# The chunked delta rule of one mixer: its 64x64 blocks held without their empty quarters

## The chip, the cores and the metric

The kernel runs on one core of a Trainium2 chip. The metric is device time in microseconds (us) from launch to the last byte written; lower is better. The kernel before took 2299.62 us, the median of three runs (2299.19 to 2301.99).

## The reference

Two models' blocks stand one behind the other on 512 tokens of width 1024, all in float32: four layers (pooling, short convolution, latent attention, pooling), then a hybrid mixer and a gated feed-forward layer. The change is in the mixer, in its gated delta rule: 4 heads, key and value size 128, chunks of 64 tokens.

```python
def gated_delta_rule(q, k, v, g, beta):          # chunks of C = 64 tokens, 8 chunks
    g = jnp.cumsum(chunks(g), axis=-1)
    decay = jnp.where(causal, jnp.exp(gdiff), 0.0)            # C x C for each chunk
    L = jnp.where(strict, einsum('bhnid,bhnjd->bhnij', k_beta, k) * decay, 0.0)
    rhs = jnp.concatenate([v * beta[..., None], k_beta * jnp.exp(g)[..., None]], axis=-1)
    sol = triangular_solve(L + jnp.eye(C), rhs, left_side=True, lower=True, unit_diagonal=True)
    u, w = sol[..., :dv], sol[..., dv:]
    a_intra = einsum('bhnid,bhnjd->bhnij', q, k) * decay
    ...
    def step(state, xs):                                      # 8 steps, one after the other
        v_new = u_c - w_c @ state
        o = qd_c @ state + a_c @ v_new
        state = state * jnp.exp(gl_c) + kd_c.T @ v_new
```

## The kernel before, in words

Every projection is a stream of tiles. A tile is 128 output features by 512 tokens: 24 TensorE products (L665 to L667) of 128x512, three for each of 8 blocks of a weight split into a high and a low part. SyncE loads the weights, ScalarE makes the high parts (L1212), GpSimd the low parts (L594), in a ring of four buffers. Each engine has its own instruction order, written out by hand; semaphores of the mixer count named steps (`mixer_steps`), and an engine waits for the count of the step that it needs.

In the mixer the delta rule works on pairs of chunks: 512 tokens are 4 blocks of 128 tokens, and each block's 128x128 matrix has two 64x64 chunk matrices on its diagonal and zeros in the other two quarters. One step handles one head: four blocks side by side, 128 partitions by 512 columns, one PSUM bank.

`delta_products` on TensorE sets groups of four heads between single projection tiles: `bg` spreads the summed gate over 128 partitions (L907), `vt` and `kt` turn values and keys (L914), `g1` is keys by scaled keys (L916), `g2` keys by queries (L916). VectorE makes the decay exponent from `bg` (L2004), ScalarE its exponential (L1456). VectorE multiplies `g1` into the lower matrix and takes from it the start of the inverse (L2021, L2023, L2024), and multiplies `g2` (L2030).

`inverse` then builds the inverse of the triangular matrix by doubling the block size from 2 to 64, levels 1 to 5. First `x1` turns `xt` (L914) and `bg2` spreads the gate again (L907). In each level and for each head TensorE makes `y` from `e_mat` and `x_mat` (L916, bank in `proj`); ScalarE copies it into `y_mat` (L1483); TensorE makes `p`, that is two products, one into `aux` and one into `proj` (L916); VectorE subtracts them from `x_mat` (L2046) and `xt` (L2048), and masks the next level's `e_mat` while `p` is under way (L2042). Level 5 has only the product into `aux` and no `e_mat`. `wt` multiplies `vf` by the inverse (L916), and ScalarE stores it negated (`nw`, L1495). No projection tile stands between the steps of `inverse`.

Last comes a loop over 8 chunks that is interleaved with two softmax attentions, all products in one TensorE order: attention scores (L1006), `new_values` (L1018 the inverse by the values, L1021 the product with the state, head by head in turn), turned probabilities (L1057), outputs (L1033, L1037), state update (L1043), attention values (L1071), sums (L1084).

A product in plain float32 is recorded as two weight loads and two matmuls; a "record" below is one of them. The projection's products, on split operands, are one record each, as are the turns at L914.

Of the kernel before, what the change touches and what calls it, by code (L numbers as in the profile page):

```python
# [24 lines left out]
P = 128  # L25
# [52 lines left out]
for _name, _n in (("levels", LEVELS * P), ("mask_t", P), ("dist", 4 * P), ("dist_swa", 2 * P)):  # L78
    CONSTS2[_name] = _at
    _at += _n  # L80
# [78 lines left out]
def mixer_steps():  # L159
# [10 lines left out]
    act += each("egl", "edt") + each("vb") + each("kd") + each("xc") + each("eg")  # L170
# [93 lines left out]
def program(nc, x_in, stream, params_in, consts_in, consts2_in, pos_in, out, phases):  # L264
    ctx = ExitStack()
    with ctx:
# [18 lines left out]
        x_mat = sb("x_mat", [P, 4, 4, P], F32, late)  # L285
        y_mat = sb("y_mat", [P, 4, 4, P], F32, late)
        e_mat = sb("e_mat", [P, 4, 4, P], F32, late)
        v_tok = sb("v_tok", [P, 4, 3, P], F32, late)
        eg = y_mat
# [81 lines left out]
        l_mat = kb.rearrange("p h (b k) -> p h b k", k=P)  # L371
# [14 lines left out]
        xt = sb("xt", [P, 4, 4, P], F32, over)  # L386
# [89 lines left out]
        def level(l):  # L476
            return consts2[:, l * P:l * P + P].unsqueeze(1).broadcast_to([P, 4, P])
# [4 lines left out]

        def decay_of(h):
            return blocks_of(decay[:, h, :])
# [159 lines left out]
        def _(pe):  # L644
# [273 lines left out]

            def tiles(n):
                for _ in range(n):  # L920
                    products(tile.n % BANKS, 8, of_x)

            def delta_products():
# [22 lines left out]
                for h in HEADS:  # L946
                    pe.wait_ge(mix_dve, DVE_STEP["kb", h])
                    made(spread_row(h, 0, 32 + h), ("bg", h))
                tiles(1)
                for h in HEADS:  # L950
                    pe.wait_ge(mix_act, ACT_STEP["egl", h])
                    made(per_block(h, 0, None, lambda blk: vf[:, h, blk * P:blk * P + P], turn=True), ("vt", h))
# [5 lines left out]
                for h in HEADS:  # L958
                    pe.wait_ge(mix_act, ACT_STEP["kd", h])
                    made(per_block(h, 0, lambda blk: kf[:, h, blk * P:blk * P + P],  # L960
                                   lambda blk: kb[:, h, blk * P:blk * P + P]), ("g1", h))
                tiles(1)
                for h in HEADS:
                    pe.wait_ge(mix_dve, DVE_STEP["lt", h])
                    made(per_block(h, 0, lambda blk: kf[:, h, blk * P:blk * P + P],
                                   lambda blk: qf[:, h, blk * P:blk * P + P]), ("g2", h))
                tiles(1)

            def inverse():

                for h in HEADS:
                    pe.wait_ge(mix_dve, DVE_STEP["at", h])
                    made(per_block(h, 0, None, lambda blk: xt[:, h, blk, :], turn=True), ("x1", h))
# [3 lines left out]
                for l in range(1, LEVELS):  # L977
                    for h in HEADS:
# [31 lines left out]
            def new_values(c):  # L1010
# [14 lines left out]
            def output_and_update(c, last_value):  # L1025
# [10 lines left out]
                for h in HEADS:  # L1036
                    mm = pe.matmul(banks(1)[:, h * CHUNK:h * CHUNK + CHUNK], vnew[r:r + CHUNK, h * P:h * P + P],  # L1037
                                   blocks_of(kf[:, h, :])[r:r + CHUNK, blk, r:r + CHUNK],
# [159 lines left out]
        def _(act):  # L1198
# [186 lines left out]
            def hybrid_mixer():  # L1385
# [88 lines left out]
                for h in HEADS:  # L1474
                    act.wait_ge(mix_pe, PE_STEP["x1", h])
                    made(act.activation(x_mat[:, h, :, :], blocks_of(head_bank(h, 0)), ACT.Copy), ("xc", h))
                for h in HEADS:
                    act.wait_ge(mix_pe, PE_STEP["bg2", h])
                    made(act.activation(eg[:, h, :, :], blocks_of(head_bank(h, 1)), ACT.Exp), ("eg", h))
# [13 lines left out]
                for h in HEADS:  # L1493
                    act.wait_ge(mix_pe, PE_STEP["wt", h])
                    made(act.activation(vf[:, h, :], head_bank(h, 0), ACT.Copy, scale=-1.0), ("nw", h))  # L1495
# [154 lines left out]
        def _(dve):  # L1650
# [256 lines left out]
            def hybrid_mixer():  # L1907
# [91 lines left out]
                mask_t = consts2[:, CONSTS2["mask_t"]:CONSTS2["mask_t"] + P]  # L1999
# [19 lines left out]
                for h in HEADS:  # L2019
                    dve.wait_ge(mix_pe, PE_STEP["g1", h])  # L2020
                    made(dve.tensor_tensor(l_mat[:, h, :, :], blocks_of(head_bank(h, 0)), decay_of(h), ALU.mult), ("lt", h))  # L2021

                    link(dve.tensor_tensor(xt[:, h, :, :], l_mat[:, h, :, :], level(0), ALU.mult))  # L2023
                    made(dve.scalar_tensor_tensor(xt[:, h, :, :], xt[:, h, :, :], -1.0,  # L2024
                                                  con("ident", P).unsqueeze(1).broadcast_to([P, 4, P]),
                                                  ALU.mult, ALU.add), ("xt0", h))
# [374 lines left out]
```

## Time and profile before

| what | us |
|---|---|
| profiled execution, its own time | 2300.2 |
| its span | 2298.4 |
| median of three runs | 2299.62 |
| TensorE matmuls busy | 2224.7 (97%) |
| VectorE busy | 1168.0 (51%) |
| ScalarE busy | 894.3 (39%) |
| GpSimd busy | 1066.4 (46%) |

In the rows below PE is TensorE's matmuls, PEld its weight loads, DVE is VectorE, ACT is ScalarE, POOL is GpSimd. A matmul row has the rows and columns of the array that it uses before its output's shape: `64*128` is 64 rows by 128 columns. Matmuls are pipelined, so the time that a matmul costs in a stream is the distance from its start to the next one's start, which is shorter than its own duration.

### The profile page before, as it was taken

What the parts mean: (1) busy time and instruction counts of PE and PEld (TensorE: products, weight loads), DVE (VectorE), ACT (ScalarE), POOL (GpSimd) and SP (SyncE); (2) the same over time, 40 slices, a digit from 0 to 9 for tenths busy, and PEclk for the clock granted to TensorE, in tenths of its full rate; (3) what the DMA queues carried; (4) which work ended last, traced back from release to release, by engine and by line L of the source; (5) the groups of instructions that cost most, each with busy time, mean ns of one, the idle gap of its engine ahead of it and who ended that gap; (6) DMA issues with size and microseconds to landing.
All of it is one profiled execution on the core that took longest, in us unless ns stands there. A gap on an engine that the chain in (4) does not pass through costs nothing.

```text
span 2298.4 us, 32107 instructions
## 1 busy us (share of the span) xinstructions
PE 2224.7 (97%) x10384; PEld 1799.7 (78%) x10384; DVE 1168.0 (51%) x1538; ACT 894.3 (39%) x1567; POOL 1066.4 (46%) x789
## 2 busy tenths in 40 slices
PE   8999999999999999999999999999999888999996
PEld 6788888888888887777787788878798666878885
DVE  7842234444432553555338523367684448888513
ACT  4243333434433344444332444334635433332322
POOL 5654444454454444444446544445302333555553
PEclk9999999999999999999999999999999889999998
DMA  3232322222222232111122322322200021223232
GB/s 136 92 110 91 101 92 101 91 100 94 98 97 95 97 101 75 63 56 56 65 92 92 101 98 94 101 98 92 71 22 1 1 73 56 91 91 100 101 109 92
DMA packets 53642, 194.45 MB, mean 85 GB/s; under 512 B 6080, under 2 KB 6336, under 8 KB 53568
## 3 DMA queue, kind: packets, MB, share of 16 engines
q1 hardware_dynamic: 52560, 191.13, 24.7%
q10 hardware_dynamic: 1008, 2.33, 0.3%
q8 instruction: 47, 0.77, 0.1%
q14 instruction: 27, 0.22, 0.0%
HBM read 191.34 MB, written 2.10 MB: 84 GB/s over the span
## 4 chain that ended last, share of the span: by engine, by line
PE 71%; issue 17%; POOL 9%; DVE 2%; ACT 1%; POOLq 0%; ACTq 0%; DVEq 0%
PE proj L665 18%; PE proj L666 18%; PE proj L667 18%; POOL w_lo L594 9%; PE aux L799 2%; PE proj L824 1%; PE proj L916 1%; PE aux L916 1%; PE proj L753 1%; PE proj L755 1%; PE proj L754 1%; PE aux L802 1%; PE aux L810 1%; PE proj L1018 0%; PE aux L1006 0%
## 5 line engine op out<-in xcount | busy, mean ns | idle before, releaser
L594 POOL TENSOR_TENSOR w_lo<-w_stage,w_hi 128x512 fp32r<-128x512 f32 x716 | 989.9, 1391 | 1029.0 <-ACT w_hi L1212 1028.3
L1212 ACT ACTIVATE w_hi<-w_stage 128x512 fp32r<-128x512 f32 x716 | 438.1, 627 | 770.1 <-PE proj L667 701.8
L665 PE MATMUL proj<-xh,w_hi 128*128 128x512 f32 x1696 | 671.2, 396 | 11.8 <-POOL w_lo L594 9.7
L666 PE MATMUL proj<-xl,w_hi 128*128 128x512 f32 x1696 | 662.7, 391 | 0.0
L667 PE MATMUL proj<-xh,w_lo 128*128 128x512 f32 x1696 | 662.4, 391 | 0.0
L665 PEld LDWEIGHTS proj<-xh,w_hi 128*128 128x128 f32 x1696 | 319.2, 188 | 94.2 <-POOL w_lo L594 22.2
L666 PEld LDWEIGHTS proj<-xl,w_hi 128*128 128x128 f32 x1696 | 319.5, 188 | 66.7 <-issue 2.4
L667 PEld LDWEIGHTS proj<-xh,w_lo 128*128 128x128 f32 x1696 | 319.4, 188 | 66.9
L665 PE MATMUL proj<-act_h,w_hi 128*128 128x512 f32 (+1 forms) x840 | 327.6, 390 | 0.6 <-POOL w_lo L594 0.6
L667 PE MATMUL proj<-act_h,w_lo 128*128 128x512 f32 (+1 forms) x840 | 327.3, 390 | 0.0
L666 PE MATMUL proj<-act_l,w_hi 128*128 128x512 f32 (+1 forms) x840 | 327.3, 390 | 0.0
L665 PEld LDWEIGHTS proj<-act_h,w_hi 128*128 128x128 f32 x840 | 157.8, 188 | 34.7 <-issue 1.0
L667 PEld LDWEIGHTS proj<-act_h,w_lo 128*128 128x128 f32 x840 | 157.8, 188 | 32.7
L666 PEld LDWEIGHTS proj<-act_l,w_hi 128*128 128x128 f32 x840 | 157.8, 188 | 32.3
L1289 ACT ACTIVATE act_h<-prod 128x512 f32 (+1 forms) x102 | 64.5, 632 | 257.7 <-DVE prod L2150 130.7
L1671 DVE TENSOR_TENSOR ssum<-ssum,sq 128x512 f32<-128x512 f32 x64 | 62.0, 969 | 152.2 <-ACT sq L1218 151.5
L1712 DVE TENSOR_TENSOR x_res<-proj,x_res 128x512 f32 x32 | 22.1, 692 | 218.4 <-PE proj L667 217.1
L1751 DVE TENSOR_TENSOR act_l<-prod,act_h 128x512 f32 (+1 forms) x102 | 82.0, 804 | 84.8 <-ACT act_h L1289 84.8
L2156 DVE TENSOR_TENSOR z<-proj,rstd 128x512 f32<-128x512 f32 x32 | 22.1, 692 | 112.7 <-PE proj L667 111.9
L632 POOL TENSOR_SCALAR probs<-probs,soft 128x256 f32<-128x256 f32 (+3 forms) x32 | 30.4, 962 | 105.3 <-DVE soft L2059 105.3
L608 POOL TENSOR_SCALAR pr<-pr,small 128x128 f32<-128x128 f32 (+3 forms) x32 | 40.8, 1274 | 76.1 <-DVE small L1851 76.1
L1336 ACT ACTIVATE pr<-aux,small 128x128 f32<-128x128 f32 (+3 forms) x64 | 33.2, 524 | 53.1 <-DVE small L1844 53.1
(311 smaller groups left out, 2427.7 us busy)
## 6 DMA issues: line engine op xcount, KB each, us to landing
w_stage<-stream SPq DMA_DIRECT2D x358, 512.0 KB, 3.3
out<-x_res SPq DMA_DIRECT2D x4, 512.0 KB, 2.6
x_res<-x SPq DMA_DIRECT2D x2, 512.0 KB, 8.7
consts_sb<-consts ACTq DMA_DIRECT2D x1, 832.0 KB, 4.5
x_res<-x ACTq DMA_DIRECT2D x1, 512.0 KB, 7.8
x_res<-x SPq DMA_DIRECT2D x1, 256.0 KB, 3.4
x_res<-x ACTq DMA_DIRECT2D x1, 256.0 KB, 5.4
pos_i<-pos ACTq DMA_DIRECT2D x1, 256.0 KB, 2.6
```

Of the source, the lines that this page charges most:

```text
L594: pool.tensor_tensor(w_lo[:, at, :], w_stage[:, at, :], w_hi[:, at, :].bitcast(F32), ALU.subtract).then_inc(stage_free, 1)
L608: pool.tensor_scalar(pr[:, qb % 2, 0, 0:w], pr[:, qb % 2, 0, 0:w], stat(INVERSE, qb)[:, 0:1], None, ALU.mult).then_inc(probs_done, 1)
L665: pe.matmul(o, w_hi[:, slot, cols], hi, start=(b == 0), stop=False)
L666: pe.matmul(o, w_hi[:, slot, cols], lo, start=False, stop=False)
L667: mm = pe.matmul(o, w_lo[:, slot, cols], hi, start=False, stop=(b == blocks - 1))
L799: pe.matmul(score_banks(qb, w)[:, h, :], qn[:, p % 2, h, q], kn[:, p % 2, h, 0:w], start=True, stop=False)
L916: mm = pe.matmul(o, stationary(blk), moving(blk), start=True, stop=True)
L1212: act.activation(w_hi[:, u % RING, :], w_stage[:, u % RING, :], ACT.Copy).then_inc(hi_done, 1)
L1289: act.activation(act_h[:, slot, :], prod[:, :], ACT.Copy).then_inc(ah_done, 1)
L1336: e = act.activation(pr[:, qb % 2, h, 0:w], score_banks(qb, w)[:, h, :], ACT.Exp, bias=stat(BIAS, qb)[:, h:h + 1], scale=SCALE, accum_out= ...
L1671: dve.tensor_tensor(total[:, :], total[:, :], sq[:, (sqs.n - 1) % 2, :], ALU.add).then_inc(ssum_done, 1)
L1751: dve.tensor_tensor(act_l[:, slot, :], prod[:, :], act_h[:, slot, :].bitcast(F32), ALU.subtract).then_inc(al_done, 1)
```

## The change

Each chunk's 64x64 matrix is now kept alone. Of a block of 128 tokens the first chunk lies on partitions 0 to 63 and the second on 64 to 127, both in the same 64 columns, so a head takes 128 partitions by 256 columns. `x_mat`, `y_mat`, `e_mat`, `xt`, the level masks and the decay have this half width. Every 128x128 product of these steps becomes two 64x64 products, one on each half of the partitions. `bg` is made in this form by two products; the decay exponent is made by two VectorE operations of 256 columns a head in place of four of 128. `x1` can no longer be one turn of a block and becomes products with an identity. `wt` multiplies each half into its own bank. The exponential of the chunk ends (`egl`) moves behind `bg2`, and `eg` has a buffer of its own. In the chunk loop the product of the inverse with the values reads 64 rows where it read 128.

```diff
+            def per_chunk(h, b, stationary, moving):
+                for blk in range(4):
+                    for r in (0, CHUNK):
+                        mm = pe.matmul(compact(head_bank(h, b))[r:r + CHUNK, blk, :], stationary(blk, r), moving(blk, r),
+                                       start=True, stop=True)
+                return mm
...
-                    made(spread_row(h, 0, 32 + h), ("bg", h))
+                    for r in (0, CHUNK):
+                        at = CONSTS["ident"] + 32 + h
+                        mm = pe.matmul(compact(head_bank(h, 0))[r:r + CHUNK, :, :],
+                                       consts[0:64, at:at + 1].broadcast_to([64, CHUNK]),
+                                       rows[0:64, :].rearrange("p (b r k) -> p b r k", r=2, k=CHUNK)[:, :, r // CHUNK, :],
+                                       start=True, stop=True)
+                    made(mm, ("bg", h))
...
-                    made(per_block(h, 0, lambda blk: kf[:, h, blk * P:blk * P + P],
-                                   lambda blk: kb[:, h, blk * P:blk * P + P]), ("g1", h))
+                    made(per_chunk(h, 0, tokens_of(kf, h), tokens_of(kb, h)), ("g1", h))
...
-                    made(per_block(h, 0, None, lambda blk: xt[:, h, blk, :], turn=True), ("x1", h))
+                    made(per_chunk(h, 0, chunk_of(xt, h), ident_of), ("x1", h))
...
-                        made(per_block(h, 1, lambda blk: e_mat[:, h, blk, :], lambda blk: x_mat[:, h, blk, :]), (f"y{l}", h))
+                        made(per_chunk(h, 1, chunk_of(e_mat, h), chunk_of(x_mat, h)), (f"y{l}", h))
...
-                        mm = per_block(h, 0, lambda blk: y_mat[:, h, blk, :], lambda blk: xt[:, h, blk, :])
+                        mm = per_chunk(h, 0, chunk_of(y_mat, h), chunk_of(xt, h))
                         if l < LEVELS - 1:
-                            mm = per_block(h, 1, lambda blk: xt[:, h, blk, :], lambda blk: y_mat[:, h, blk, :])
+                            mm = per_chunk(h, 1, chunk_of(xt, h), chunk_of(y_mat, h))
...
-                    made(per_block(h, 0, lambda blk: blocks_of(vf[:, h, :])[:, blk, :],
-                                   lambda blk: xt[:, h, blk, :]), ("wt", h))
+                    for blk in range(4):
+                        for i in range(2):
+                            r = CHUNK * i
+                            mm = pe.matmul(compact(head_bank(h, i))[:, blk, :], blocks_of(vf[:, h, :])[r:r + CHUNK, blk, :],
+                                           xt[r:r + CHUNK, h, blk, :], start=True, stop=True)
+                    made(mm, ("wt", h))
...
-                    mm = pe.matmul(o, xt[:, h, blk, r:r + CHUNK], vbeta[:, h, blk, :], start=(h == 0), stop=(c == 0),
+                    mm = pe.matmul(o, xt[r:r + CHUNK, h, blk, :], vbeta[r:r + CHUNK, h, blk, :], start=(h == 0), stop=(c == 0),
...
-                    made(act.activation(egl[:, h, :], head_bank(h, 0)[:, CHUNK - 1::CHUNK], ACT.Exp), ("egl", h))
-                    made(act.activation(decay[:, h, :], decay[:, h, :], ACT.Exp), ("edt", h))
+                    made(act.activation(decay_of(h), decay_of(h), ACT.Exp), ("edt", h))
...
-                        made(act.activation(y_mat[:, h, :, :], blocks_of(head_bank(h, 1)), ACT.Copy), (f"yc{l}", h))
+                        made(act.activation(y_mat[:, h, :, :], compact(head_bank(h, 1)), ACT.Copy), (f"yc{l}", h))
...
-                    for blk in range(4):
-                        ins = dve.scalar_tensor_tensor(decay_of(h)[:, blk, :], head_bank(h, 0)[:, blk * P:blk * P + P],
-                                                       cols[:, blk, 32 + h:33 + h], mask_t, ALU.subtract, ALU.add)
-                    made(ins, ("dt", h))
+                    link(dve.tensor_tensor(decay_of(h), compact(head_bank(h, 0)),
+                                           cols[:, :, 32 + h:33 + h].broadcast_to([P, 4, CHUNK]), ALU.subtract))
+                    made(dve.tensor_tensor(decay_of(h), decay_of(h), mask_t, ALU.add), ("dt", h))
```

On TensorE, at level 1 of the inverse, the program before has for one head the product `y` (`x_mat,e_mat`) and the two products of `p`:

```order
L916 MATMUL proj<-x_mat,e_mat 128x128 [waits mix_dve,mix_act]
L916 MATMUL proj<-x_mat,e_mat 128x128 x3
L916 MATMUL aux<-xt,y_mat 128x128 [waits mix_act]
L916 MATMUL aux<-xt,y_mat 128x128 x3
L916 MATMUL proj<-y_mat,xt 128x128 x4
```

The changed program has at the same place, its lines being L933:

```order
L933 MATMUL proj<-x_mat,e_mat 64x64 [waits mix_dve,mix_act]
L933 MATMUL proj<-x_mat,e_mat 64x64 x7
L933 MATMUL aux<-xt,y_mat 64x64 [waits mix_act]
L933 MATMUL aux<-xt,y_mat 64x64 x7
L933 MATMUL proj<-y_mat,xt 64x64 x8
```

Twelve products of 128x128 have become twenty-four of 64x64; the waits are the same.

On TensorE in the chunk loop, at chunk 1, the program before has between two score products (L1006) the new values, where `xt` and `vf` are the operands of the inverse and of the state:

```order
L1006 MATMUL aux<-a_kv,a_q 128x256
L1018 MATMUL proj<-vbeta,xt 64x128 [waits mix_dve]
L1021 MATMUL proj<-state,vf 64x128
L1018 MATMUL proj<-vbeta,xt 64x128
L1021 MATMUL proj<-state,vf 64x128
L1018 MATMUL proj<-vbeta,xt 64x128
L1021 MATMUL proj<-state,vf 64x128
L1018 MATMUL proj<-vbeta,xt 64x128
L1021 MATMUL proj<-state,vf 64x128
```

The changed program has the same order, its lines being L1045, L1057 and L1060:

```order
L1045 MATMUL aux<-a_kv,a_q 128x256
L1057 MATMUL proj<-vbeta,xt 64x128 [waits mix_dve]
L1060 MATMUL proj<-state,vf 64x128
L1057 MATMUL proj<-vbeta,xt 64x128
L1060 MATMUL proj<-state,vf 64x128
L1057 MATMUL proj<-vbeta,xt 64x128
L1060 MATMUL proj<-state,vf 64x128
L1057 MATMUL proj<-vbeta,xt 64x128
L1060 MATMUL proj<-state,vf 64x128
```

Nothing has moved here; what the rows don't show is that L1057 now reads 64 partitions where L1018 read 128, while L1060 reads 128 as L1021 did.

## Rows read from the trace of the kernel before

**Rows 1.** The page: the chain that ended last, by engine.

```profile
PE 71%; issue 17%; POOL 9%; DVE 2%; ACT 1%; POOLq 0%; ACTq 0%; DVEq 0%
```

**Rows 2.** Windows (from:to us, length, busy time of each engine, clock, DMA).

```profile
1626.00:1684.90 58.90, 58.61 (x290) 44.95 (x289) 43.48 (x74) 25.93 (x64) 18.64 (x14) 1.00 0.21 72
1684.90:1739.00 54.10, 53.84 (x480) 53.65 (x480) 40.79 (x56) 18.48 (x33) 0.00 (x0) 1.00 0.01 1
1756.00:1812.00 56.00, 52.59 (x424) 43.96 (x422) 24.16 (x88) 31.44 (x93) 25.08 (x26) 0.94 0.01 1
1776.00:1779.00 3.00, 3.00 (x15) 3.00 (x16) 0.61 (x4) 0.00 (x0) 1.41 (x2) 0.51 0.00 0
```

**Rows 3.** The chain that ended last, in the inverse (start us, us, what, records).

```profile
1694.97 4.47 PE proj L916 x40
...
1705.69 4.47 PE proj L916 x40
...
1731.59 7.16 PE aux L916 x64
```

**Rows 4.** Timeline, one level of the inverse (start, us, engine, line, idle before).

```profile
1713.83 0.69 DVE L2046 TENSOR_TENSOR x_mat<-x_mat,proj 128x512 f32<-128x512 f32 x1 [0.38 <-PE proj L916]
...
1718.29 0.60 ACT L1483 ACTIVATE y_mat<-proj 128x512 f32<-128x512 f32 x1 [6.12 <-PE proj L916]
1718.85 2.87 DVE L2042 TENSOR_TENSOR e_mat<-mixed,consts_sb 128x512 f32<-128x512 f32 x4
```

**Rows 5.** Groups by form (busy us, mean ns, idle before).

```profile
L2066 DVE CUSTOM_DVE_ANT_0 aux<-aux,bias_b 128x512 f32<-128x512 f32 x2 | 1.3, 715 | 0.0
L2066 DVE CUSTOM_DVE_ANT_0 aux<-aux,bias_b 128x256 f32<-128x256 f32 x2 | 0.8, 449 | 0.0
L1541 ACT ACTIVATE mixed<-proj 128x256 f32<-128x256 f32 x6 | 2.3, 383 | 4.1 <-PE proj L1037 4.1
L937 PE MATMUL aux<-consts_sb,rows 68*128 68x68 f32 x4 | 0.4, 226 | 0.0
```

**Rows 6.** Timeline of TensorE in front of the inverse.

```profile
1637.37 3.70 PE L907 MATMUL aux<-rows,consts_sb 64*128 64x512 f32 x8
...
1661.02 3.73 PE L916 MATMUL aux<-mixed,kf 128*128 128x128 f32 x32
...
1679.07 1.91 PE L914 MATMUL aux<-consts_sb,xt 128*128 128x128 f32 x16
...
1684.90 1.35 PE L916 MATMUL proj<-x_mat,e_mat 128*128 128x128 f32 x10 [0.30 <-DVE qf L2037]
```

**Rows 7.** Timeline of TensorE at two seams: with and without another array shape.

```profile
1637.05 0.39 PE L667 MATMUL proj<-xh,w_lo 128*128 128x512 f32 x1
1637.37 0.69 PE L907 MATMUL aux<-rows,consts_sb 64*128 64x512 f32 x1
...
1646.36 0.39 PE L667 MATMUL proj<-xh,w_lo 128*128 128x512 f32 x1
1646.59 0.38 PE L914 MATMUL aux<-consts_sb,vf 128*128 128x128 f32 x2
```

**Rows 8.** Timeline of TensorE: runs of records in five array shapes.

```profile
1622.19 0.41 PE L937 MATMUL aux<-consts_sb,rows 68*128 68x68 f32 x4
...
1741.67 0.49 PE L1006 MATMUL aux<-a_kv,a_q 64*128 64x128 f32 x4
1742.09 1.09 PE L1018 MATMUL proj<-vbeta,xt 128*64 128x128 f32 x8
...
1752.59 1.00 PE L1033 MATMUL proj<-qf,state 128*128 128x64 f32 x8
...
1813.78 1.09 PE L1071 MATMUL proj<-probs_t,v_tok 128*64 128x128 f32 x16
```

**Rows 9.** Line L1021 (ns min/median/max), and who waited for it (us, times).

```profile
L1021 PE MATMUL proj<-state,vf x56: 272/273/421, 1748.4 to 1806.2; 128*64 128x128 f32 x56
...
  ACT vnew L1537: 19.0, 7
```

More of the change, by code:

```diff
@@ L77 @@
 _at = 0
-for _name, _n in (("levels", LEVELS * P), ("mask_t", P), ("dist", 4 * P), ("dist_swa", 2 * P)):
+for _name, _n in (("levels", LEVELS * CHUNK), ("mask_t", CHUNK), ("ident_c", CHUNK), ("dist", 4 * P), ("dist_swa", 2 * P)):
     CONSTS2[_name] = _at
@@ L169, in mixer_steps @@
     act = each("zs") + ["tanh", "e1", "nega", "ln"] + each("sk") + each("sq") + each("rk") + ["cexp"] + each("rq") + ["ckd"]
-    act += each("egl", "edt") + each("vb") + each("kd") + each("xc") + each("eg")
+    act += each("edt") + each("vb") + each("kd") + each("xc") + each("egl", "eg")
     for l in range(1, LEVELS):
@@ L385, in program @@
         b_k = sb("b_k", [P, 2, S], F32, over)
-        xt = sb("xt", [P, 4, 4, P], F32, over)
+        xt = sb("xt", [P, 4, 4, CHUNK], F32, over)
+        sb("behind_xt", [P, 4, 4, CHUNK], F32, over)
         squares_over = ExitStack()
@@ L476, in level, with compact, lower_of, within_of @@
         def level(l):
-            return consts2[:, l * P:l * P + P].unsqueeze(1).broadcast_to([P, 4, P])
+            return consts2[:, l * CHUNK:l * CHUNK + CHUNK].unsqueeze(1).broadcast_to([P, 4, CHUNK])
         def head_bank(h, i):
             return (aux if i == 0 else proj)[:, h, :]
+        def compact(ap):
+            return ap[:, 0:4 * CHUNK].rearrange("p (b k) -> p b k", k=CHUNK)
         def decay_of(h):
-            return blocks_of(decay[:, h, :])
+            return compact(decay[:, h, :])
+        def lower_of(h):
+            return compact(kb[:, h, :])
+        def within_of(h):
+            return compact(kf[:, h, :])
         def pair_of(k):
@@ L917, in per_block, with ident_of, chunk_of, tokens_of @@
                 return mm
+            def per_chunk(h, b, stationary, moving):
[4 more added lines that the diff above has]
+                return mm
+            def ident_of(blk, r):
+                at = CONSTS["ident"] + r
+                return consts[r:r + CHUNK, at:at + CHUNK]
+            def chunk_of(ap, h):
+                return lambda blk, r: ap[r:r + CHUNK, h, blk, :]
+            def tokens_of(ap, h):
+                return lambda blk, r: ap[:, h, blk * P + r:blk * P + r + CHUNK]
             def tiles(n):
@@ L1475, in hybrid_mixer @@
                     act.wait_ge(mix_pe, PE_STEP["x1", h])
-                    made(act.activation(x_mat[:, h, :, :], blocks_of(head_bank(h, 0)), ACT.Copy), ("xc", h))
+                    made(act.activation(x_mat[:, h, :, :], compact(head_bank(h, 0)), ACT.Copy), ("xc", h))
                 for h in HEADS:
                     act.wait_ge(mix_pe, PE_STEP["bg2", h])
+                    made(act.activation(egl[:, h, :], head_bank(h, 1)[:, CHUNK - 1::CHUNK], ACT.Exp), ("egl", h))
                     made(act.activation(eg[:, h, :, :], blocks_of(head_bank(h, 1)), ACT.Exp), ("eg", h))
@@ L1494, in hybrid_mixer @@
                     act.wait_ge(mix_pe, PE_STEP["wt", h])
-                    made(act.activation(vf[:, h, :], head_bank(h, 0), ACT.Copy, scale=-1.0), ("nw", h))
+                    for i in range(2):
+                        ins = act.activation(vf[:, h, :].rearrange("p (b r k) -> p b r k", r=2, k=CHUNK)[:, :, i, :],
+                                             compact(head_bank(h, i)), ACT.Copy, scale=-1.0)
+                    made(ins, ("nw", h))
                 for blk in range(4):
@@ L2020, in hybrid_mixer @@
                     dve.wait_ge(mix_pe, PE_STEP["g1", h])
[L2021 to L2026, printed above, removed]
+                    made(dve.tensor_tensor(lower_of(h), compact(head_bank(h, 0)), decay_of(h), ALU.mult), ("lt", h))
+                    link(dve.tensor_tensor(xt[:, h, :, :], lower_of(h), level(0), ALU.mult))
+                    made(dve.scalar_tensor_tensor(xt[:, h, :, :], xt[:, h, :, :], -1.0, ident_c, ALU.mult, ALU.add), ("xt0", h))
                 take_tile()
@@ L2041, in hybrid_mixer @@
                             dve.wait_ge(mix_pe, PE_STEP[f"y{l}", h])
-                            made(dve.tensor_tensor(e_mat[:, h, :, :], l_mat[:, h, :, :], level(l + 1), ALU.mult), (f"e{l + 1}", h))
+                            made(dve.tensor_tensor(e_mat[:, h, :, :], lower_of(h), level(l + 1), ALU.mult), (f"e{l + 1}", h))
                     for h in HEADS:
@@ L2370, in pack @@
     c2 = np.zeros((P, NCONSTS2), np.float32)
+    pc, cc = p % CHUNK, np.arange(CHUNK)[None, :]
     for l in range(LEVELS):
         s = 1 << l
-        c2[:, l * P:l * P + P] = (p // (2 * s) == c // (2 * s)) & (p // s % 2 == 0) & (c // s % 2 == 1)
-    c2[:, CONSTS2["mask_t"]:CONSTS2["mask_t"] + P] = np.where((p // CHUNK == c // CHUNK) & (c >= p), 0.0, -1e30)
+        c2[:, l * CHUNK:l * CHUNK + CHUNK] = (pc // (2 * s) == cc // (2 * s)) & (pc // s % 2 == 0) & (cc // s % 2 == 1)
+    c2[:, CONSTS2["mask_t"]:CONSTS2["mask_t"] + CHUNK] = np.where(cc >= pc, 0.0, -1e30)
+    c2[:, CONSTS2["ident_c"]:CONSTS2["ident_c"] + CHUNK] = pc == cc
     k = np.arange(4 * P)[None, :]
```

29 lines of the change are left out of this document (14 added, 15 removed).

## The prediction, as it was put on record

> **What bounds the kernel now.** I read the page's last chain first: 71% of it is TensorE [rows 1]. An average says nothing of the stage that changes, so I cut the mixer into windows [rows 2]. In front of the inverse (1626 to 1684.9) TensorE is busy 58.6 of 58.9 us and VectorE 43.5. In the inverse (1684.9 to 1739) TensorE is busy 53.8 of 54.1 us, VectorE 40.8, ScalarE 18.5, GpSimd and DMA idle. The chain agrees: it runs through L916 without another engine's work, one level from 1694.97 to 1705.69, 10.72 us [rows 3]. The timeline says what the others do: VectorE waits 0.38 us for each pair of products and ScalarE 6.12 us for a level's first `y` [rows 4]. So time taken off TensorE counts in both stretches, until VectorE is the bound. In the chunk loop TensorE is busy 52.6 of 56 us [rows 2]; ScalarE waits 19.0 us in total for the seven last products of the new values [rows 9], so that loop follows TensorE too.
>
> **What one record costs.** L916 has 8 records a head and product. A level is 12 such products (4 `y`, 8 in `p`), 96 records in 10.72 us: 0.112 us each, 0.89 us a product. In the runs below I take off the last record's own length, about 0.27 us [rows 9], and divide by the steps. L1033, 64 moving columns on a full array, still takes (1.00 - 0.27) / 7 = 0.10 us a record [rows 8]: with 128 stationary columns the load binds, fewer moving columns alone gain nothing. L937, with 68 columns on both sides, has (0.41 - 0.23) / 3 = 0.06 us a record [rows 5, 8]. So a 64x64 record should cost half of 0.112, 0.056 us; but there are twice as many. The gain is whether two halves run side by side. L1018, all products in one column half, takes (1.09 - 0.27) / 7 = 0.117 us a record; L1071, the same shape with its products in alternate column halves, takes (1.09 - 0.27) / 15 = 0.055 [rows 8]. Column halves overlap fully, within one bank. L1006 alternates row halves, in two banks: its 4 records take (0.49 - 0.27) / 3 = 0.07 us each, less than the 0.11 of their 128 columns [rows 8]. Row halves overlap too. Quarters that differ in both are not in the trace. I take full overlap: 0.056 us a pair of records, 0.45 us a head and product. From the other side: no overlap, 0.89 us, as before.
>
> **What a change of array shape costs.** L907 (64 rows) starts 0.32 us after L667, L914 (128 rows) only 0.23 after its L667 [rows 7]: 0.09 us for the seam. The Trainium skill, "TensorEngine Tiling (Array Packing)", Key Properties, says that changing the tiling mode drains the engine, and it lists 64x64 and 128x64 as different modes. The trace agrees where it has seams, and has none of this kind; by the rule the new seam costs like the rest, without it the chunk-loop term below is 0.
>
> **The sum, by part.**
> - `bg`: 8 records of L907 in 3.70 us, 0.43 each [rows 6]. Now 8 pairs in column halves with 256 columns, 0.215 each, 1.7 in all: -1.9.
> - `g1`, `g2`: 32 records of 0.112, 3.57 us each, of which `g1` stands in [rows 6]. Now 32 pairs of 0.056, 1.8, and two seams of 0.09 in and out: -1.6 each, -3.2. Upper bound: no gain, +0.2 each.
> - `x1`: 16 turns, one record each, 0.109 apart, 1.74 us [rows 6]; now 64 records in pairs, 1.8, and a seam: +0.15.
> - Cover: these gains need VectorE to keep up. Its `g1` work falls from 12 operations of 0.69 to 12 of about 0.42, and the decay from 16 operations of 128 columns to 8 of 256; its slack before is 15 us of 59 [rows 2]. I charge nothing.
> - Start of level 1: TensorE waited 0.30 us for `qd` [rows 6]. VectorE still takes `b_v` at the same distance and then does `e1` at half width, but `qd` is full width behind `eg`, and ScalarE now does 4 `egl` before them: +0.1.
> - Levels 1 to 4: TensorE 12 products of 0.45, 5.4 us. VectorE has 12 operations. Its 512-column one takes 0.69, and 2.87 us for four gives 0.04 between [rows 4]. One operation at two widths differs by 0.266 us for 256 columns [rows 5], so 0.69 - 0.27 + 0.04 = 0.46 each, 5.5 a level. ScalarE's copies take 0.38 [rows 5], 1.5 a level. VectorE becomes the bound by a hair: 4 x (5.5 - 10.72) = -20.9. From the other side: 0.
> - Level 5 and `wt`: before, 3.58 for `y` and 7.16 for `p` and `wt` [rows 3], 10.7. Now 1.8, 1.8, a seam, and for `wt` 32 pairs whose loads have 128 columns, 0.112 each, 3.6 as before: 7.3, so -3.4. If the row halves of `wt` did not overlap: 3.6 more.
> - `nw`: the last head has two copies of 0.38 in place of one of 0.60: +0.2.
> - Chunk loop: in chunks 1 to 7, L1057 (64 rows) and L1060 (128 rows) alternate, so 7 seams more a chunk, 49 in all. At 0.09 that is 4.4 us. At 1776 the new values run at a granted clock of 0.51, its lower level, 1.2 GHz [rows 2]; if some three chunks do and a seam costs double there, 6.3. It lies on the path [rows 9]; TensorE's 3.4 us idle may take some. I take +5.0, bounds 0 and 6.3.
>
> Sum: -1.9 - 3.2 + 0.15 + 0.1 - 20.9 - 3.4 + 0.2 + 5.0 = -24. The profiled execution took 2300.2 us (span 2298.4 and 1.8 around it), 0.6 over the median of the runs. 2300.2 - 24 = 2276.
>
> **Rivals.**
> 1. The new seam is free, because 64 and 128 rows with 64 columns are no change for the array. For: L1018 and L1021 alternate today without a loss, but both read 128 rows. 2271 us.
> 2. The quarters do not overlap, since both write one bank from different rows. For: L1006's row halves go to two banks [rows 8], and `wt` was given two banks. Against: L1071 overlaps in one bank, though with all rows. Then the levels gain nothing, `x1` costs 3.6 + 0.1 against 1.74 (+1.9), and only `bg` and `g1`, `g2` gain: -1.9 - 3.2 + 1.9 + 0.1 + 0.2 + 0.1 + 5.0 = +2.2, 2302 us, within what can be told from no change. The Trainium skill, "TensorEngine Tiling (Array Packing)", Gotcha 1, says that different row tiles cannot access the same PSUM bank simultaneously. By it this rival holds; no row here shows such a pair in one bank.
> 3. In part: pairs overlap, but each record has a fixed cost of 0.04. TensorE then has 1088 small records in `x1`, `g1`, `g2`, `y` and `p` (64 + 128 + 4 x 192 + 128): 43.5 us against 58.9 before, so -15.4, with -1.9 for `bg` and +5.8 for seams and small terms: -11.5, 2289 us.
> 4. The other side, slower: TensorE's issue sets a fixed cost for every record, above what array time asks. L1071 shows only that 0.055 is possible, L937 0.06 [rows 8]. At 0.055: 1088 x 0.055 = 59.8 against 58.9, +0.9, and +3.9 for the rest, +4.8: 2305 us. It decides from 0.051 a record, where the sum is nil. For: the pairs need four instructions in 0.056 us, twice the rate that any row shows. Against: nothing in the trace runs short of instructions. The Trainium skill, "TensorE: Matmul & The Clock Gate", Part 2, gives an issue cost of about 62 ns for each MATMUL when the hardware decoder is off; L1071's 0.055 over 16 records is below it, so the trace speaks against it here; by it the time would be an estimated 2313.
> 5. The clock: if quarter products leave the grant at 1.2 GHz through the inverse, pairs cost double, a level is 10.7 again, `wt` 3.6 longer, `y` and `p` of level 5 as before: about 2304. Against: L1018 and L1071 use half the array and the stretch from 1756 still has 0.94 [rows 2].
>
> **How the numbers follow.** Forecast 0.64; rival 1, 0.08; rival 3 and what lies between, 0.12; rival 2, 0.07; rival 4, 0.06; rival 5, 0.03. A measurement tells 0.2%, 4.6 us, from no change. Faster: 0.64 + 0.08 + 0.12 = 0.84. Rival 2 and most of 5 are within it: 0.09. Slower: 0.07. The range goes from 2267 (no seams, and VectorE's gaps smaller) to 2290 (rival 3); above it lie rivals 2, 4 and 5 with 0.16. The forecast's own range is 2272 to 2281, from the seam's bounds 4.4 to 6.3 and some 0.3 us a level.
>
> **What would show it.** The inverse, from the first `y` to the end of `wt`, takes about 29 us, not 54; a level lasts 5.5 us and VectorE has almost no idle time in it. `y` of a head has 16 records in pairs some 7 ns apart, a pair each 0.056 us. `bg` takes 1.8 us, `g1` and `g2` 1.8 to 2.0. The new values of a chunk take about 0.65 us more than before at full clock, each start 0.2 after the last where the line changes. Wrong would be records of a head evenly 0.056 apart (rival 2), pairs wider than 0.1 (4), a granted clock near 0.5 in the inverse (5), or no wider starts at L1060 (1).

## The result, and the profile after

| | before | after |
|---|---|---|
| median of 7 runs, us | 2300.44 (2299.09 to 2303.37) | 2309.35 (2307.83 to 2314.11) |
| profiled execution, us (span) | 2300.2 (2298.4) | 2309.35 (2307.6) |
| mean granted clock of TensorE | 0.986 | 0.970 |
| first score product of the chunk loop, us | 1741.7 | 1715.0 |
| chunk loop, us | 70.7 | 104.5 |

After over before is 1.0038 (95%: 1.0029 to 1.0048): slower by 8.9 us. The forecast was 2276, its range 2267 to 2290; the prediction was wrong, in sign too. Two executions, one of experiment 5 (5765.8 us) and one of the kernel before that was run beside experiments 5 to 7 (7805.6 us), lie far outside all others and enter no ratio.

All of the new work gained nearly what was forecast, and the loop behind it lost more. In the profiled spans: the loop begins 26.7 us earlier, lasts 33.8 longer, the stretch behind it 1.9 longer (14.6 to 16.5), all else 0.2. Sum: -26.7 + 33.8 + 1.9 + 0.2 = +9.2, which is 2307.6 - 2298.4.

The page of the kernel after: busy time and share, the chain by engine, and the granted clock in 40 slices. They answer to [rows 1]. Behind them stands the clock line of the kernel before.

```profile
PE 2235.4 (97%) x10984; PEld 1790.0 (78%) x10984; DVE 1147.8 (50%) x1530; ACT 888.5 (39%) x1571; POOL 1067.0 (46%) x789
...
PEclk9999999999999999999999999999996689999998
...
PE 71%; issue 17%; POOL 9%; DVE 2%; ACT 1%; POOLq 0%; ACTq 0%; DVEq 0%
```

```profile
PEclk9999999999999999999999999999999889999998
```

Neither the share of TensorE nor the chain tells the two kernels apart. The line of the clock does: slices of 57.7 us, of which the two with a 6 cover 1731 to 1846.

**Windows.** From and to (us), length, then busy time and instructions of TensorE, its weight loads, VectorE, ScalarE and GpSimd, granted clock, DMA share, GB/s. After, to set beside [rows 2]: the stretch before the inverse, the inverse, the chunk loop, and what follows the loop.

```profile
1628.80:1681.07 52.27, 52.27 (x402) 39.79 (x401) 36.68 (x65) 22.60 (x60) 17.74 (x14) 1.00 0.23 71
1681.07:1712.00 30.93, 30.40 (x961) 30.07 (x960) 26.55 (x56) 14.73 (x37) 0.00 (x0) 1.00 0.02 4
1715.00:1819.50 104.50, 99.72 (x513) 71.13 (x512) 32.15 (x116) 39.17 (x119) 29.88 (x32) 0.65 0.00 1
1819.50:1836.00 16.50, 13.37 (x75) 8.51 (x75) 4.50 (x13) 8.36 (x18) 6.07 (x4) 0.62 0.00 0
```

The same two stretches before:

```profile
1741.70:1812.40 70.70, 65.42 (x513) 54.64 (x512) 31.17 (x116) 39.15 (x119) 30.07 (x32) 0.93 0.00 1
1812.40:1827.00 14.60, 10.86 (x75) 7.12 (x74) 4.85 (x13) 8.51 (x18) 5.56 (x4) 0.77 0.00 1
```

The inverse takes 30.9 us, not 54.1, at a full clock. The loop has the same instructions on every engine (513 products, 116, 119 and 32) and takes 104.5 us at a mean clock of 0.65, not 70.7 at 0.93. The clock has two levels, 1.2 and 2.4 GHz, so a mean of 0.65 is (1 - 0.65) x 2 x 104.5 = 73 us at the lower one; before it was 10 us. VectorE, ScalarE and GpSimd are as busy as before, to 1 us each, so none of them has more to do.

**Where the clock falls.** Before, the loop has three stretches at the lower level:

```profile
1748.70:1752.10 3.40, 3.40 (x18) 2.74 (x15) 0.80 (x4) 0.63 (x2) 1.72 (x2) 0.50 0.00 0
1776.00:1779.40 3.40, 3.40 (x18) 3.07 (x18) 0.61 (x4) 0.00 (x0) 1.41 (x2) 0.51 0.00 0
1796.50:1799.90 3.40, 3.40 (x18) 3.07 (x17) 1.21 (x5) 0.35 (x1) 2.37 (x2) 0.50 0.00 0
```

After, it has the same three, and a fourth begins at 1818.4, 1 us before its end:

```profile
1722.80:1753.50 30.70, 30.70 (x134) 22.31 (x132) 8.00 (x32) 10.91 (x36) 8.85 (x11) 0.50 0.00 1
1763.80:1780.90 17.10, 17.10 (x76) 11.48 (x74) 4.28 (x16) 4.71 (x15) 4.68 (x6) 0.50 0.00 1
1791.10:1815.00 23.90, 23.90 (x101) 16.72 (x101) 5.71 (x17) 6.07 (x16) 5.88 (x7) 0.50 0.00 1
```

In both kernels the three begin within 2 us of the start of the new values of chunks 1, 4 and 6, and 0.5 to 2.1 us after TensorE has waited: 1.76 us for the state in chunk 1, and 0.89 to 0.96 us for ScalarE before chunks 4 and 6. So these falls were there before the change. What it changes is how long the clock stays down: 3.4 us each time before, 30.7, 17.1 and 23.9 us after. In these stretches TensorE reads as busy throughout, 30.70 of 30.70 us, so its busy share does not show them.

**The chain of waits** after (start, us, what): `bg`, `g1`, `x1`, a level's `y` and `p` and the next, the last `p`, and the new values in the loop at either level. To set beside [rows 3, 6].

```profile
1638.15 1.87 PE aux L981 x16
1660.14 2.02 PE aux L933 x64
1675.50 2.01 PE aux L933 x64
...
1692.88 2.33 PE proj L933 x80
...
1698.48 2.33 PE proj L933 x80
...
1706.41 1.87 PE aux L933 x64
...
1736.52 0.61 PE proj L1057 x2
1737.14 0.62 PE proj L1060 x2
...
1753.77 0.36 PE proj L1060 x2
1754.14 0.36 PE proj L1057 x2
```

`bg` takes 1.87 us (before 3.63), `g1` 2.02 (3.57), `x1` 2.01 (1.74). A level is 1698.48 - 1692.88 = 5.60 us; before it was 10.72. Eighty records in 2.33 us are 0.029 us each, 0.058 a pair. A head's products use two quarters of the array (rows and columns 0 to 63, and rows and columns 64 to 127), and these overlap fully, in one bank.

**Timeline** of TensorE and its neighbours in the inverse after, to set beside [rows 4] (in brackets the idle time before, and its releaser).

```profile
1683.33 0.68 PE L933 MATMUL proj<-x_mat,e_mat 64*64 64x64 f32 x16 [0.53 <-ACT y_mat L1522]
...
1693.91 1.78 ACT L1522 ACTIVATE y_mat<-proj 128x256 f32<-128x256 f32 x4 [2.92 <-PE proj L933]
1694.37 1.80 DVE L2081 TENSOR_TENSOR e_mat<-mixed,consts_sb 128x256 f32<-128x256 f32 x4
1695.02 0.66 PE L933 MATMUL aux<-xt,y_mat 64*64 64x64 f32 x16
```

VectorE's half-width operations come 0.45 us apart, under TensorE's 0.47 a head: TensorE binds a level, by as little as VectorE was thought to.

**Timeline at the seams** after: two array shapes in the new values, full clock. The second column of a row is its busy time; the price is in the distance of the starts.

```profile
1755.15 0.43 PE L1060 MATMUL proj<-state,vf 128*64 128x128 f32 x2
1755.51 0.43 PE L1057 MATMUL proj<-vbeta,xt 64*64 64x128 f32 x2
1755.87 0.43 PE L1060 MATMUL proj<-state,vf 128*64 128x128 f32 x2
```

The same place before:

```profile
1757.94 0.38 PE L1021 MATMUL proj<-state,vf 128*64 128x128 f32 x2
1758.15 0.38 PE L1018 MATMUL proj<-vbeta,xt 128*64 128x128 f32 x2
1758.37 0.38 PE L1021 MATMUL proj<-state,vf 128*64 128x128 f32 x2
```

0.36 us from start to start, not 0.22: 0.14 us a seam, 6.9 us for 49. That is a fifth of what the loop lost; the other 26.9 us came with 63 us more at the lower clock, 0.43 us for each of them.

### The profile page after: what moved, and what is told of

The parts are those of the page before. It is cut to its first block, busy times and chain, and to the rows that moved or that the text cites. A ratio compares the mean times of both kernels' runs of the same rounds, so it can differ in the third digit from the quotient of the medians.

```text
span 2307.6 us, 33303 instructions
## 1 busy us (share of the span) xinstructions
PE 2235.4 (97%) x10984; PEld 1790.0 (78%) x10984; DVE 1147.8 (50%) x1530; ACT 888.5 (39%) x1571; POOL 1067.0 (46%) x789
## 4 chain that ended last, share of the span: by engine, by line
PE 71%; issue 17%; POOL 9%; DVE 2%; ACT 1%; POOLq 0%; ACTq 0%; DVEq 0%
PE proj L676 18%; PE proj L677 18%; PE proj L678 18%; POOL w_lo L605 9%; PE aux L810 2%; PE proj L835 1%; PE proj L764 1%; PE proj L766 1%; PE proj L765 1%; PE aux L813 1%; PE aux L821 1%; PE proj L1057 1%; PE proj L933 1%; PE aux L933 1%; PE proj L1060 1%
```

## The experiments

Three theories stood at first. S: the seams themselves keep the clock low. R: products that read only 64 rows do it. L: the lighter TensorE stretch ahead of the loop lets the clock fall. A seam is a change of array shape from one product to the next. The edits are shown in short: arguments are left out, and `...` marks a gap. The loop's row of windows is shown for each; its columns are those above. A row is of the one profiled execution, the times are of all.

**1. After, with the two kinds of product in two groups** (one new seam a chunk, not seven).

```
 -  for h in HEADS:  pe.matmul(o, xt[r:r+CHUNK, h, blk, :], vbeta[r:r+CHUNK, ...]); if c: pe.matmul(o, vf, state)
 +  for h in HEADS:  pe.matmul(o, xt[r:r+CHUNK, h, blk, :], vbeta[r:r+CHUNK, ...])
 +  for h in HEADS if c else ():  pe.matmul(o, vf, state)
```

> The changed kernel with the new values in another order: the four products of the inverse with the values first, then the four with the state, in place of head by head in turn. One extra change of array shape a chunk in place of seven; the same products, rows and columns. Known so far: the changed kernel takes 2309.35 us, its inverse ends 26.8 us earlier than before and its chunk loop takes some 33 us longer, with a granted clock near 0.5 for most of it. Theory S (the seams slow the loop and hold the clock down): the clock recovers after each dip as before, 7 x 0.14 = 1 us of seams are left, 2300.4 - 26.8 + 1 = about 2275 us. Rival L (the lighter stretch ahead of the loop, or the seams not at all, leaves the clock low): only the seams' own time goes, 6 x 7 x 0.17 = 7 us, about 2302 us. Rival R (products on 64 rows keep the clock low): the same about 2302 us.

```profile
1713.30:1793.00 79.70, 74.70 (x512) 61.27 (x512) 31.45 (x116) 39.19 (x119) 30.29 (x32) 0.82 0.01 1
```

Measured 2281.86 us (2274.03 to 2289.39), 0.9921 of before (0.989 to 0.9951). Order alone turns the change into a gain. The loop is 25 us shorter than after, still 9 longer than before, with 29 us at the lower clock. L alone can't say why an order matters. But S had said 2275, with the clock of before, and that came only in part: the four runs lie between 2274 and 2289.

**2. Before, with only the 64-row products** (no change to the inverse).

```
 -  mm = pe.matmul(o, xt[:, h, blk, r:r + CHUNK], vbeta[:, h, blk, :], ...)
 +  mm = pe.matmul(o, xt[r:r + CHUNK, h, blk, r:r + CHUNK], vbeta[r:r + CHUNK, h, blk, :], ...)
```

> The kernel before with one edit: the product of the inverse with the values reads the chunk's 64 rows of both operands, in the old 128-wide layout (the rows left out hold zeros). The inverse and all else are as before. Theory S: the whole loss of the loop appears without the gain of the inverse, about 2300.4 + 35 = 2335 us, and the granted clock of the loop is near 0.5 for most of it. Rival L: the clock is as in the kernel before and only the seams are paid, 49 x 0.14 = 7 us, about 2307 us. Rival R: about 2335 us as S.

```profile
1741.00:1852.00 111.00, 106.83 (x512) 76.96 (x512) 31.40 (x116) 39.32 (x119) 30.06 (x32) 0.59 0.00 1
```

2337.01 us, 1.0158 (1.0142 to 1.0175). The whole loss is there with the old inverse in front of it: L falls. (The profiled execution is the longest of the four, 4.1 us above the median, so the row may show the loop too long by as much.)

**3. Before, with the 64-row products and in two groups.** Experiment 2 and the grouping of experiment 1.

```
 +  for h in HEADS:  pe.matmul(o, xt[r:r+CHUNK, h, blk, r:r+CHUNK], vbeta[r:r+CHUNK, ...])
 +  for h in HEADS if c else ():  pe.matmul(o, vf, state)
```

> The kernel before with the 64-row products and the grouped order together: 64 rows read, one extra seam a chunk. Theory S: 7 x 0.14 = 1 us, about 2301.5 us, clock of the loop as before. Rival R (it is the 64 rows, not the seams): the clock stays low, 2325 us or more. Rival L: 2301.5 us as S.

```profile
1740.70:1820.60 79.90, 74.61 (x512) 60.97 (x512) 31.32 (x116) 39.18 (x119) 30.13 (x32) 0.82 0.00 1
```

2309.81 us, 1.0048 (1.0031 to 1.0065). The same loop as in experiment 1, 79.9 and 79.7 us at 0.82: what stands in front makes no difference in these two. The time is neither that of S (2301.5) nor that of R (2325 or more).

**4. After, in two groups of two heads** (three new seams a chunk).

```
 +  for group in ((0, 1), (2, 3)):
 +      for h in group:  pe.matmul(o, xt[r:r+CHUNK, ...], vbeta[r:r+CHUNK, ...])
 +      for h in group if c else ():  pe.matmul(o, vf, state)
```

> The changed kernel with the new values in two groups of two heads: three extra seams a chunk in place of seven. A dose between. Theory S with the clock following the dose: 21 x 0.14 = 3 us of seams and, if the clock recovers as with one seam, about 2277 us; if three seams are enough to hold it down in part, 2280 to 2295 us. Rivals L and R: 2309.35 less 4 x 7 x 0.17 = 5 us, about 2305 us.

```profile
1714.60:1795.50 80.90, 75.90 (x513) 59.13 (x512) 32.41 (x116) 39.16 (x119) 29.81 (x32) 0.83 0.00 1
```

2290.49 us over ten runs, but from 2281.11 to 2308.01; 0.998 (0.9956 to 1.0005). The profiled run is the shortest of them. The mean clocks of the spans go with the times: 0.983 in the run of 2281.11 us, 0.969 in that of 2308.01. Here the grant differs from run to run, and the row is of a run 9.4 us below the median, so it says little of a dose; the table at the end has the medians.

**5. Before, in two groups** (same products, 128 rows, no new seam).

```
 -                    if c:  mm = pe.matmul(o, vf[:, h, toks], state[:, h, :], ...)
 +                for h in HEADS if c else ():  mm = pe.matmul(o, vf[:, h, toks], state[:, h, :], ...)
```

> The kernel before with the new values in the grouped order (four products of the inverse, then four with the state), all on 128 rows: no seam is added or removed. It is the control for the order. Known: both kernels with 64-row products in grouped order (one extra seam a chunk) had a granted clock near half for about 27 us of the loop, against 10 us before, and the loop took 80.7 us against 70.3. Theories S (seams) and R (64 rows): no difference, about 2300 us. If the grouped order itself costs the clock: about 2310 us.

```profile
1741.60:1813.50 71.90, 66.64 (x513) 55.67 (x512) 31.17 (x116) 39.40 (x119) 30.05 (x32) 0.91 0.00 1
```

2301.23 us, 1.0004 (0.9994 to 1.0014). The order as such costs nothing, so experiment 1's gain came by its seams.

**6. After, without a 64-row product in the loop.** GpSimd, idle in the inverse, makes two copies of the finished inverse with the other chunk's rows set to zero, and the loop reads all 128 rows.

```
 +  pool.tensor_scalar(xt_odd, xt, consts2[half + 1], None, ALU.mult)     # behind the last xt
 +  pool.tensor_scalar(xt, xt, consts2[half], None, ALU.mult)             # behind wt
 -  mm = pe.matmul(o, xt[r:r + CHUNK, h, blk, :], vbeta[r:r + CHUNK, h, blk, :], ...)
 +  mm = pe.matmul(o, (xt_odd if r else xt)[:, h, blk, :], vbeta[:, h, blk, :], ...)
```

> The changed kernel with the chunk loop's array shapes of before: GpSimd, idle there, makes two zero-filled copies of the finished inverse (first chunks and second chunks, 128 partitions by 1024 columns each), so that the product with the values reads 128 rows again. No seam and no 64-row product is added; the inverse keeps its gain. Theories S and R: the loop takes 70 to 72 us, 2300.4 - 26.8 + 0.5 = about 2274 us. Rival L (the lighter stretch ahead of the loop holds the clock down): the loop takes 80 us or more, 2284 us or more.

```profile
1714.40:1784.90 70.50, 65.50 (x512) 54.80 (x512) 31.32 (x116) 39.08 (x119) 30.07 (x32) 0.93 0.01 1
```

Its timeline at the two new operations:

```profile
1708.21 2.84 POOL L642 TENSOR_SCALAR xt_odd<-xt,consts_sb 128x1024 f32<-128x1024 f32 x1 [31.33 <-DVE xt L2098]
1711.49 2.84 POOL L646 TENSOR_SCALAR xt<-xt,consts_sb 128x1024 f32<-128x1024 f32 x1 [0.43 <-PE proj L1041]
```

2272.43 us, 0.9877 (0.9861 to 0.9894). The loop is that of before to 0.2 us, at the same clock, behind the new inverse. GpSimd is done at 1714.33, before the loop's first product at 1714.4. The rest of the change is worth 28 us; what failed is the loop alone.

**7. Before, with seams between 128-row products.** The state-query products (128*128) are issued between the two kinds of new-value products (128*64), head by head.

```
        pe.matmul(o, xt[:, h, blk, r:r + CHUNK], vbeta[:, h, blk, :], ...)
 +      if c: pe.matmul(banks(1)[...], state[:, h, :], qf[:, h, toks], ...)
        if c: pe.matmul(o, vf[:, h, toks], state[:, h, :], ...)
```

> The kernel before with seams and without 64-row products: the products of the state with the queries (full array) are taken between the new values' products (128 rows, 64 columns), head by head, seven extra changes of shape a chunk, every product reading 128 rows. Theory S: the loop slows as with the alternating 64-row products, 2330 to 2340 us, clock near half for most of it. Rival R (64-row products, not seams, hold the clock down): seams are paid at full clock only, 49 x 0.14 = 7 us, about 2307 us.

```profile
1741.70:1852.10 110.40, 104.86 (x514) 77.43 (x512) 32.27 (x116) 39.39 (x119) 29.87 (x32) 0.63 0.00 1
```

2337.36 us, 1.016 (1.0143 to 1.0177). By its rows it has eight new seams a chunk, not the seven of the expectation. No product reads 64 rows that did not before, and the loop is as long as in experiment 2: R is not needed. S stands. The edit also takes the wait for the previous chunk's output copy ahead of the new values; TensorE is idle for 110.40 - 104.86 = 5.5 us of the loop, before for 5.3, so that wait is not the loss. At full clock a head takes 0.94 us (1781.57 to 1782.51); its three products alone would take 0.22 + 0.21 + 0.22 = 0.65, so each of the two seams costs 0.14 to 0.15 us here too. (Here too the profiled execution is the longest, 5.0 us above the median.)

**8. Before, with the state-query products right behind the new values** (one new seam in some chunks, beside the group and not in it).

```
            new_values(c):  ... mm.then_inc(...)
 +              for h in HEADS if c else ():  pe.matmul(banks(1)[...], state[:, h, :], qf[:, h, toks], ...)
            output_and_update(c):
 -              for h in HEADS if c else ():  pe.matmul(banks(1)[...], state[:, h, :], qf[:, h, toks], ...)
```

> The kernel before with the products of the state with the queries moved from in front of the outputs to right behind the new values: the same products, all on 128 rows, one more change of array shape a chunk (chunks 1 to 6). What is open: the two kernels with one extra seam a chunk by 64-row products lost 10 us in the loop. Theory S (one seam a chunk is enough, since the loop sits close to the point where the clock falls): about 2310 us, 20 us or more of the loop at the low clock. Rival R (in that small dose it was the 64-row products): about 2301.5 us, 10 us at the low clock as before.

```profile
1744.10:1815.90 71.80, 66.51 (x512) 54.95 (x511) 31.26 (x116) 39.32 (x119) 30.23 (x32) 0.93 0.00 1
```

2301.85 us over ten runs, 1.001 (1.0 to 1.0019). By its rows it has a new seam in chunks 1 to 5 alone, five in all: in chunks 6 and 7 no score product stands between the new values and the turned probabilities, and the state-query products lie beside products of their own shape, as before. The clock stays, and the loop is 1.1 us longer, of which five seams at 0.14 make 0.7. The time is the one forecast for R, not for S: one seam here did not do what one seam did in experiment 3.

**9. The version of experiment 6, with one seam less.** A chunk's second set of score products moves in front of its outputs, next to products of the same shape.

```
 -  new_values(c); if b > a: attend(b); output_and_update(c, a - 4)
 +  new_values(c); output_and_update(c, a - 4, b if b > a else None)    # attend(b) before the wait on vnew
```

> The version with the half-width inverse and 128-row products in the loop (2272.4 us), with the second score product of a chunk moved from behind the new values to right in front of the outputs, which have its array shape: one seam fewer a chunk in chunks 0 to 5. Theory S: 5 x 0.14 = 0.7 us of seams less and fewer dips of the clock (each 3.4 us at half clock costs up to 1.7 us): 2267 to 2271 us. If the clock does not follow the seams: 2271.7 us. On the other side, the softmax of the second pair starts later: if its maxima or exponentials are then waited for, 2274 us or more.

```profile
1714.80:1782.60 67.80, 62.76 (x512) 53.69 (x512) 31.14 (x116) 39.13 (x119) 30.17 (x32) 0.95 0.00 1
```

2270.05 us (2269.48 to 2272.33), 0.9869 (0.9853 to 0.9886). The loop falls below that of before, and by 2.7 us against experiment 6. Five seams, in chunks 1 to 5, make 0.7 of it and 3.1 us less at the lower clock 1.3; the rest is not accounted for. It beats both kernels. As a time it is not told from experiment 6, since the two intervals overlap; 2271.7, forecast for a clock that does not follow the seams, lies within its runs.

**10. Before, in three groups** (two new seams a chunk inside the new values, all of 128 rows).

```
 +  for h in HEADS:  pe.matmul(o, xt[...], vbeta[...])
 +  for h in HEADS if c else ():  pe.matmul(banks(1)[...], state[:, h, :], qf[:, h, toks])
 +  for h in HEADS if c else ():  pe.matmul(o, vf[...], state[...])
```

> The kernel before with the new values in three groups: four products of the inverse, then the four products of the state with the queries (full array), then four products of the new values with the state; every product on 128 rows, two extra changes of shape a chunk in chunks 1 to 7. Open: one extra seam a chunk cost 1.5 us with 128-row products and 9.5 us with 64-row ones. If the number of seams or their place inside the new values is what counts (theory S in small doses): 2308 us or more, 20 us or more of the loop at the low clock. If the 64-row products add to it (R beside S): seams are paid at their own price, 2 x 7 x 0.1 to 0.14 = 1.4 to 2 us, about 2302.5 us.

```profile
1744.00:1833.20 89.20, 83.00 (x512) 65.68 (x512) 31.25 (x116) 39.14 (x119) 29.81 (x32) 0.75 0.00 1
```

2312.66 us (2309.67 to 2320.68; the profiled run is the longest, 8.0 above the median), 1.0051 (1.0033 to 1.0069). With 128 rows alone, a few seams inside the new values hold the clock down too, as S had it (2308 or more) and R had not (2302.5).

**What they show together.** New seams in the loop are set against its kernel without them (before, or for the kernels with the new inverse experiment 6); time at the lower clock is (1 - clock) x 2 x length of each row. The last column is the median of all runs less that of before in the same session, with 27.9 added for the kernels with the new inverse, which is what experiment 6 gains.

| kernel | new seams a chunk | loop, us | longer by | of which seams at 0.14 | more at lower clock, us | us lost for each | median, us slower |
|---|---|---|---|---|---|---|---|
| after | 7 | 104.5 | +34.0 | 6.9 | 63 | 0.43 | 36.8 |
| 2 | 7 | 111.0 | +40.3 | 6.9 | 81 | 0.41 | 36.9 |
| 7 | 8 | 110.4 | +39.7 | 7.8 | 72 | 0.44 | 37.0 |
| 4 | 3 | 80.9 | +10.4 | 2.9 | 18 | 0.43 | 18.3 |
| 10 | 2 | 89.2 | +18.5 | 2.0 | 35 | 0.48 | 12.3 |
| 1 | 1 | 79.7 | +9.2 | 1.0 | 19 | 0.44 | 9.7 |
| 3 | 1 | 79.9 | +9.2 | 1.0 | 19 | 0.43 | 9.7 |
| 8 | 1, in five chunks | 71.8 | +1.1 | 0.7 | 0 | | 2.4 |

Every loop that lost much is made up of the two prices, a seam's own 0.14 us and 0.41 to 0.48 us for each microsecond at 1.2 GHz. (That it is under 0.5 is presumably because not all of the loop is TensorE's.) The rows of 4 and 10 are of their shortest and longest run; by the medians the loss grows with the seams inside the new values, from one to two, three and seven, though the runs of 1, 10 and 4 spread over 15, 11 and 27 us and the kernels differ in rows. Seams bring the loss in two ways that have no pair of array shapes in common, `64*64` beside `128*64` in experiment 2 and `128*128` beside `128*64` in experiment 7; taking them out, in experiment 6, brings the gain. How they act on the clock is not shown by any record, and three things stay open. By the medians seven seams cost some 30 us through the clock, one in each chunk costs 9 inside the new values and under 2 beside them (8), so it is no rate per seam. Where the seam stands seems to matter (8 against 3), but these two differ in rows and in number of seams as well. And why single runs of one program, as in 4, get different grants.

## Why the prediction was wrong, by its own steps

- **`bg`**: predicted -1.9, measured 3.63 to 1.87, -1.8. Right.
- **`g1`, `g2`**: -3.2; 3.57 to 2.02 each, -3.1. Right; two seams included, and VectorE kept up, at no charge as forecast.
- **`x1`**: +0.15; 1.74 (what 16 such turns take in the chain) to 2.01, +0.27: 0.1 too small.
- **Start of level 1**: +0.1; the first `y` no longer waits for `qd`, but TensorE waits 0.53 us for a copy of `y` at 1683.33. Those copies stand behind four short `egl` and four `eg` in ScalarE's order. The two lines below leave -23.2 + 20.5 + 3.4 = +0.7 for it, so it was 0.6 too small.
- **Levels 1 to 4**: -20.9; 5.60 a level, so 4 x (5.60 - 10.72) = -20.5. The size was right and the bound the other one: TensorE with 0.058 us a pair, not VectorE with 0.46 an operation.
- **Level 5 and `wt`**: -3.4; `y` and `p` take four times 0.47 each, 1.87 in the chain, and `wt` stayed at 3.6, as said: 7.3 after 10.7. The whole inverse fell by 54.1 - 30.9 = 23.2 us.
- **`nw`**: +0.2; from the end of `wt` to the loop 3.0 us (1712.0 to 1715.0) after 2.7 (1739.0 to 1741.7), +0.3. Right.
- All in front of the loop: -29 predicted. The loop began 26.7 us earlier, and the run was 0.7 late at the start of the stretch already: -27.4. Experiment 6 gives the same by the median, -28.
- **Chunk loop**: +5.0 predicted, +33.8 measured. This is the step that failed, and it alone outweighs the rest. It took 49 seams at 0.09 us, 4.4 us, and added a doubling where the clock is low. Its own price was too small (0.14; the 0.09 was read at a seam in front of products that stream four times as many columns, [rows 7]), which is 2.5 us of its own. The other 26.9 came because the clock was taken as given: the mean of 0.94 in [rows 2] was carried over to a loop with a new pattern of products, and the row at 1776 with 0.51, which shows that this loop already falls to the lower level, was used only to size a seam. Bounds of 0 and 6.3 left the clock out, so the range could not hold it. What the runs showed in its place: seams inside the new values keep the clock from coming back, 73 us of the loop at the lower level against 10, and without them (experiment 6) the loop takes 70.5 us. The stretch behind the loop, 1.9 us longer at a clock of 0.62 against 0.77, has no term in the sum at all.
- **Rival 5** had the right mechanism, a lower grant, at the wrong place: the inverse with its quarter products ran at 1.00 throughout. **Rivals 2 to 4** are out, by 0.029 us a record in one bank. **Rival 1** is out by 0.36 against 0.22 us. Its figure, 2271, is what the change takes without the seams: experiment 6 measured 2272.4.

The rules of the Trainium skill that were weighed can be set against the runs. The Trainium skill, "TensorEngine Tiling (Array Packing)", Key Properties, says a change of tiling mode drains the engine. The trace agrees in that each new change costs time, 0.14 us in the new values. The Trainium skill, "TensorEngine Tiling (Array Packing)", Gotcha 1, says that different row tiles cannot access one PSUM bank simultaneously. That does not show here: the two quarters that a head's products use differ in rows, write one bank and overlap fully, 0.058 us a pair where one half-array record takes 0.055 [rows 8]. The Trainium skill, "TensorE: Matmul & The Clock Gate", Part 2, gives some 62 ns for each MATMUL with the hardware decoder off. It is not seen here either, at 0.029 us a record.

## What to carry over

When an edit changes the array shape of a few products among others, look at what alternates: seven seams a chunk cost this loop 7 us by themselves and 27 more through the clock, which is more than a rewritten inverse gained. Read the granted clock of the stretch, not TensorE's busy share, and where a stretch already touches the lower level, price the case that it stays there (here 0.41 to 0.48 us for each microsecond). Group products by shape, or pad with zeros on an idle engine: the 5.7 us of GpSimd in experiment 6 delayed nothing, and the kernel kept its 28 us.

## What the runs showed of the hardware

- Alternating array shapes held the granted clock at 1.2 GHz for 73 to 91 us of loops of 104 to 111 us while TensorE was busy 95 to 96% of them; the same loops without the alternation had 7 to 13 us of it. Both kernels fall to it at the same three places, just behind a wait of TensorE; without the alternation it lasted 3.4 us each time, with it 17 to 31 us.
- With few seams the clock is not a property of the program alone: ten runs of experiment 4 took 2281 to 2308 us, while the 14 of before and after in the first comparison stayed within 0.3%.
- 64x64 quarter products, in pairs and in one bank, run 0.029 us apart over 80 records, about half the 0.055 of half-array records [rows 8], so a record has no fixed cost above 0.029 us here.
